# Which side of a matmul the weights take: gate sections and branch projections of a hybrid retention and attention step

## The chip, the cores and the metric

The kernel runs on one core of one Trainium2 chip. The metric is the time of one execution in device microseconds (us). A core has TensorE (PE, with PEld for the load of a stationary side), VectorE (DVE), ScalarE (ACT), GpSimd (POOL), SyncE (SP, which issues the DMAs here), a scratch memory of 128 partitions, and PSUM banks that matmuls write.

## The reference, cut to what matters

One layer runs over 640 tokens of 1024 channels: 128 of a prompt and 512 latent ones. The part that the change touches is the mixer. The experts follow it.

```python
def mixer(h, ...):
    rq, rk, rv, rg, dq, dk, dv, gr, gd = jnp.split(h @ w_in, IN_SPLITS, axis=-1)
    ...
    ret_out = (silu(rg) * o_r) @ w_ret_o          # o_r: retention, normed
    ...
    diff_out = o_d.reshape(B, T, DIFF_V_W) @ w_diff_o   # o_d: differential attention, 8 heads, normed
    merged = jax.nn.sigmoid(gr) * ret_out + jax.nn.sigmoid(gd) * diff_out
    return merged @ w_o, dk, dv, s_f, s_b

# trunk_layer
x = x + g1 * mix
h2 = rmsnorm(x, n2) * (1.0 + sc2) + sh2
x = x + g2 * hier_moe(h2, ...)    # 32 experts, two for each token
```

## The kernel before

**Tiles and products.** The tokens are five tiles of 128 (NT; tile PT = 4 is the prompt). A weight matrix of 1024 rows is read in sections of 512 columns (SECTIONS: rq ... gr0, gr1, gd0, gd1, dq1, dk1, dv1, wr0, wr1, wd0, wd1, wo0, wo1), each in two half sections of 256 columns (hh). One half section is 1 MB, has two buffers in turn, and is split for precision: ScalarE casts it to fp32r (w_high, L1366), VectorE subtracts that from the original (w_low, L1729); the plan calls the pair "cv". The left sides h (normed input), o (retention), od (attention) and m (merged) are split in the same way into whole, high (L1339) and low (L1668), the plan's "split". A left side is made from transposes of four 128x128 blocks on TensorE ("T4", L915), copied out of PSUM with a scale per channel.

A product (plan: "mm", section, tile, half) is 24 matmuls at L882: for each of eight slices of 128 input channels high by high, high by low and low by high. The stationary side is the transposed tile of tokens, the moving side 256 columns of weights, and the result has the tokens on the partitions. Products and T4s alternate between two PSUM banks, so each waits for the copy of the one before the last.

**The order.** A list written by hand, `plan` (L357 to L468), sets the order, and each engine walks through it in its own queue. The function attention(half, work) (L402) handles four of the eight heads in 20 steps, one for each head and tile: scores of this step ("S"), transposes of the probabilities of the last step ("AT", L1050, copied at L1400), then the items of `work` that fall to this step, the preparation of the next head (three T4s in a head's steps 1 to 3), and the product with the values of the last step ("PV", L1066). Behind the scores VectorE takes the maxima (L1793 to L1795), ScalarE the exponentials (L1393). `work` is spread evenly over the 20 steps by its number of products:

```python
share[max(k - 1, 0) * len(mine) // products].append(item)
```

The first half (414 to 603 us) has the 40 products of gr and gd as its work. ScalarE takes their tanh (L1324), and SP stores each result, 128 KB, in a DRAM buffer (gate_out, L654). Then come the sections dq1, dk1, dv1 (to 690 us). The second half (to 845 us) has the 20 products of wr, with the o splits of tile t+1 behind the first section's product of tile t. SP brings back a gate for each (load_gate, L662), and VectorE writes (1 + tanh) x product into `merge` (L1636). At the end of wr1 SP asks for all gates of the attention branch at once, 2.5 MB (gd_t, L755).

**Behind the attention** (att_end, where SP also asks for the residual rows and the experts 0 and 1) stand the od transposes, those of tiles 0 and 1 ahead and those of 2 to 4 between the first five products of wd; then the rest of wd, where VectorE multiplies with the gate and adds to `merge` (L1646, L1649). The gated-merge tiles are then transposed in the same way (ten T4s, "m", with the factor 0.5) between the first products of wo; then wo1, the router, and 32 experts whose weights arrive by DMA. At the last product of wo1 SP asks for the experts 2 and 3 (L758). A product of w_o that opens the section waits for its tile's splits:

```python
if s in ("rq", "wr0", "wd0", "wo0") and hh == 0:
    pe.wait_ge(x_split, split_n[(kind, t, 1)])
```

The function final_engine (L471) gives the copy out of PSUM to ScalarE or VectorE: wr, wd and wo to VectorE, T4s of left sides by turns.

## Time and profile before

| | us |
|---|---|
| median of 3 runs (lowest, highest) | 1314.54 (1313.31, 1319.37) |
| the profiled execution | 1315.77 |
| its span in the profile | 1313.9 |
| TensorE busy | 1131.1 |
| VectorE busy | 495.6 |
| ScalarE busy | 403.5 |
| GpSimd busy | 92.4 |

The span runs from the first to the last recorded instruction of the profiled execution. "Busy" is the time in which an engine worked on an instruction that the profile counts. The chain of waits is followed back from the last instruction, each time to what released it. A bracket behind an instruction of a timeline gives the idle time before it and the instruction that ended it.

### The profile page before, as it was taken

Reading aid. Unit: us, or ns where it says so; the run is one execution under the profiler, and the core shown is the slowest. Engines: PE = TensorE matmul, PEld = TensorE weight load, DVE = VectorE, ACT = ScalarE, POOL = GpSimd, SP = SyncE. Lnnn points to the kernel's source line nnn. Section 1 sums busy time; section 2 is a strip of 40 time slices with the busy share of each in tenths; the row PEclk is TensorE's granted clock in tenths of the full one; section 3 lists DMA queues with packets and bytes.
Section 4 is the critical chain, followed back from the end, with each engine's and each line's share of the span. In section 5 each row is a group of like instructions: output and inputs, shape, how many; then the busy total and the mean of one; then the engine's idle time right before and its main releaser. Section 6 shows DMA issues by size and latency. Waiting matters only on the chain.

```text
span 1313.9 us, 19321 instructions
## 1 busy us (share of the span) xinstructions
PE 1131.1 (86%) x8087; PEld 916.5 (70%) x8087; DVE 495.6 (38%) x897; ACT 403.5 (31%) x870; POOL 92.4 (7%) x103
## 2 busy tenths in 40 slices
PE   2799999989998999999998888799895789777773
PEld 0488899989987888899996777699895333222221
DVE  0531114573343443442526545445547311111116
ACT  2532222211233545453225544421322121111113
POOL 0000001121000000000000000000001111110001
PEclk9799999999999999999999999899998799999996
DMA  8555632221321231223222111481316989999956
GB/s 302 220 170 204 224 98 65 65 60 46 105 65 41 61 93 61 75 80 109 65 73 69 53 48 49 158 319 65 129 33 254 381 346 419 421 421 421 421 241 240
DMA packets 90276, 222.32 MB, mean 169 GB/s; under 512 B 9881, under 2 KB 64962, under 8 KB 74706
## 3 DMA queue, kind: packets, MB, share of 16 engines
q1 hardware_dynamic: 85298, 209.60, 43.6%
q0 software_dynamic: 4608, 10.49, 2.1%
q8 instruction: 61, 1.00, 0.3%
q10 hardware_dynamic: 288, 1.05, 0.2%
q14 instruction: 21, 0.17, 0.0%
HBM read 206.40 MB, written 21.00 MB: 173 GB/s over the span
## 4 chain that ended last, share of the span: by engine, by line
PE 61%; DMA 13%; DVE 8%; ACT 8%; issue 6%; SPq 2%; POOL 1%; ACTq 0%; DVEq 0%; POOLq 0%
PE ps L882 39%; DMA arena<-in_moe_w_up 8%; PE ps L1112 6%; PE ps L1036 3%; PE ps L1066 3%; ACT arena L1393 2%; PE ps L1125 2%; DMA w_loaded<-in_w_in 2%; ACT w_high L1366 2%; DVE w_low L1729 2%; PE ps L1050 1%; PE ps L849 1%; DVE mx L1793 1%; DVE mx L1794 1%; DMA w_loaded<-in_w_diff_o 1%
## 5 line engine op out<-in xcount | busy, mean ns | idle before, releaser
L882 PE MATMUL ps<-w_high,h_high 128*128 128x256 f32 x1280 | 371.2, 290 | 10.0 <-DVE arena L1626 5.2
L882 PE MATMUL ps<-w_low,h_high 128*128 128x256 f32 x1280 | 364.5, 285 | 0.0
L882 PE MATMUL ps<-w_high,h_low 128*128 128x256 f32 x1280 | 364.4, 285 | 0.0
L882 PEld LDWEIGHTS ps<-w_high,h_high 128*128 128x128 f32 x1280 | 248.0, 194 | 24.5 <-ACT arena L1333 10.1
L882 PEld LDWEIGHTS ps<-w_low,h_high 128*128 128x128 f32 x1280 | 248.0, 194 | 0.2
L882 PEld LDWEIGHTS ps<-w_high,h_low 128*128 128x128 f32 x1280 | 247.8, 194 | 0.0
L1729 DVE TENSOR_TENSOR w_low<-w_loaded,w_high 128x2048 fp32r<-128x2048 f32 x44 | 100.8, 2291 | 177.7 <-ACT w_high L1366 177.7
L1112 PE MATMUL ps<-arena 128*64 128x512 f32 x512 | 121.3, 629 | 24.3 <-DMA arena<-in_moe_w_up 17.0
L1333 ACT COPY arena<-ps 128x256 f32<-128x256 f32 x100 | 37.2, 372 | 251.8 <-PE ps L882 251.8
L1112 PEld LDWEIGHTS ps<-arena 128*64 128x64 f32 x512 | 40.0, 145 | 103.5 <-issue 103.5
L1366 ACT CAST w_high<-w_loaded 128x2048 fp32r<-128x2048 f32 x44 | 84.0, 1908 | 62.0 <-DMA w_loaded<-in_w_o 37.4
L1393 ACT ACTIVATE arena<-ps,neg_mx 128x768 f32<-128x768 f32 (+1 forms) x80 | 62.8, 790 | 106.3 <-DVE neg_mx L1795 106.3
L1125 PE MATMUL ps<-arena 128*64 128x512 f32 x256 | 58.4, 598 | 9.8 <-ACT arena L1441 9.8
L1066 PE MATMUL ps<-arena 128*128 128x128 f32 x384 | 49.3, 278 | 13.3 <-ACT arena L1400 13.3
L1920 DVE SCALAR_TENSOR_TENSOR arena<-arena,ps 128x256 f32<-128x256 f32 x16 | 6.7, 421 | 141.1 <-ACT arena L1437 141.1
L1793 DVE TENSOR_REDUCE mx<-ps 128x1 f32<-128x768 f32 (+1 forms) x40 | 32.9, 822 | 71.5 <-PE ps L1036 71.5
L1066 PEld LDWEIGHTS ps<-arena 128*128 128x128 f32 x384 | 45.5, 192 | 16.1 <-ACT arena L1400 16.1
L1036 PE MATMUL ps<-arena 64*128 64x256 f32 (+2 forms) x288 | 53.9, 488 | 2.5 <-ACT arena L1282 1.5
L915 PE MATMUL ps<-const,arena 128*128 128x128 f32 x256 | 41.8, 294 | 11.2 <-POOL arena L2042 3.5
L882 PE MATMUL ps<-w_high,od_high 128*128 128x256 f32 x160 | 47.8, 299 | 4.1 <-DVE arena L1646 2.8
L882 PE MATMUL ps<-w_high,m_high 128*128 128x256 f32 x160 | 46.3, 289 | 2.0 <-DVE m_low L1668 0.8
L882 PE MATMUL ps<-w_high,o_high 128*128 128x256 f32 x160 | 46.9, 293 | 0.8 <-DVE o_low L1668 0.8
(268 smaller groups left out, 1664.0 us busy)
## 6 DMA issues: line engine op xcount, KB each, us to landing
w_loaded<-in_w_in SPq DMA_DIRECT2D x32, 1024.0 KB, 5.6
arena<-in_moe_w_gate SPq DMA_DIRECT2D x32, 1024.0 KB, 14.2
arena<-in_moe_w_up SPq DMA_DIRECT2D x32, 1024.0 KB, 20.5
arena<-in_moe_w_down SPq DMA_DIRECT2D x32, 1024.0 KB, 21.0
arena<-in_w_ada SPq DMA_DIRECT2D x24, 1024.0 KB, 5.7
gates<-arena SPq DMA_DIRECT2D x40, 128.0 KB, 1.7
arena<-y_rows SPq DMA_DIRECT2D x10, 512.0 KB, 8.2
arena<-in_x_sample SPq DMA_DIRECT2D x8, 512.0 KB, 10.8
```

The lines of the kernel that those rows point to most:

```text
L849: mm = pe.matmul(B(7)[32 * j:32 * j + 32, :], ccol[:, k, :], ada_place[ada_slot(i)][:, j * N512:(j + 1) * N512], start=(k == 0), stop=(k = ...
L882: mm = pe.matmul(out[:, 0:N256], x[:, t, k * P:(k + 1) * P], w[i % 2][:, k, :], start=(k == 0 and j == 0), stop=(k == KC - 1 and j == 2))
L915: mm = pe.transpose(out[:, k * P:(k + 1) * P], src[k], ident)
L1036: mm = pe.matmul(score[c][:, lo:hi], qT[h % 2][r, t * P:(t + 1) * P], keys, start=True, stop=True, skip_group_check=True)
L1066: mm = pe.matmul(pv_out, mixedT[s % 2][:, k * P:(k + 1) * P], v, start=(k == 0), stop=(k == 5))
L1112: mm = pe.matmul(B(bank_at)[BLK * i:BLK * (i + 1), :].rearrange("p (g f) -> p g f", g=2), xgT[slot][:, k, BLK * i:BLK * (i + 1)], w_gu[e0 ...
L1125: mm = pe.matmul(B(5 + n)[BLK * i:BLK * (i + 1), :], act_aT[slot][:, k, BLK * i:BLK * (i + 1)], w_dn[e0 + i][:, k, n * N512:(n + 1) * N512 ...
L1333: free(act.copy(dst[:, t, c0:c0 + N256], src), n)
L1366: act.copy(w_hi[i % 2][:], w_raw[i % 2]).then_inc(w_rounded, 1)
L1393: act.activation(probs[:, c, 0:n], score[c][:, 0:n], ACT.Exp, bias=neg_mx[:, s % 2, c:c + 1], scale=DH ** -0.5, accum_out=den[:, s % 2, c: ...
L1729: dve.tensor_tensor(w_lo[i % 2][:], w_raw[i % 2], w_hi[i % 2][:].bitcast(F32), ALU.subtract).then_inc(w_split, 1)
L1793: dve.tensor_reduce(mx[:, 0:1], score[0][:, 0:n], AXX, ALU.max)
```

## The change

Four kinds of section (gr, gd, wr, wd) swap the sides: 128 channels of weights are the stationary side and tokens move, 320 and 320 of them (in wd 384 and 256). A half section then has four products of 24 matmuls instead of five, and the results have channels on the partitions. The function block_of gives the channel block and the tokens of a product. The gates in DRAM, gd_t and `merge` take this layout (a gate store or load is 160 KB), so that `merge` is m's whole form: m has no T4s, its high and low parts are made from `merge` with the factor 0.5, one piece behind each product of wd.

In the plan, `work` is spread by a weight of 5 for a product and 2 for a T4. The o splits of tiles 0 to 2 stand ahead of the second half of the attention, those of tiles 3 and 4 behind its first product. The od T4s of heads 0 to 3 (half 0) with their splits become the last items of the attention's second half; the others stand behind it, ahead of the first product of wd (tiles 0 to 2) and behind it (3 and 4). The matmuls of a product are in the order high by high, low x by high w, high x by low w. The scale and shift rows of the second norm are asked for at the end of wd1 instead of behind the last m T4. Some buffers move to other places of the arena (a gate buffer holds 320 columns; scale2, shift2, h2, the weights of one expert slot, the gathered rows and the router's scratch lie elsewhere).

```diff
-        for kind, whole_kb, high_kb in (("h", 158, 118), ("o", 138, 118), ("od", 118, 178), ("m", 178, 138)):
-            left[kind] = (split_at(kind + "_whole", whole_kb, NT, D, F32), split_at(kind + "_high", high_kb, NT, D),
-                          split_at(kind + "_low", whole_kb, NT, D))
-        rv, gd_t = tiles(138, NT, D), tiles(138, NT, D)
+        for kind, whole_kb, high_kb in (("h", 158, 118), ("o", 138, 118)):
+            left[kind] = (split_at(kind + "_whole", whole_kb, KC, TOK, F32), split_at(kind + "_high", high_kb, KC, TOK),
+                          split_at(kind + "_low", whole_kb, KC, TOK))
+        merge = cols_of(158)
+        left["m"] = (merge, split_at("m_high", 138, KC, TOK), split_at("m_low", 158, KC, TOK))
+        left["od"] = (split_at("od_whole", 118, NT, D, F32), split_at("od_high", 178, NT, D), split_at("od_low", 118, NT, D))
+        rv, gd_t = tiles(138, NT, D), cols_of(138)
...
-        gates_dram = nc.dram_tensor("gates", [2, P, NT, D], F32).ap()
+        gates_dram = nc.dram_tensor("gates", [2, P, KC, TOK], F32).ap()
...
+        BY_COLUMN = ("gr", "gd", "wr", "wd")
+        LAST = lambda s: 3 if s[:2] in BY_COLUMN else PT
+
+        def block_of(s, j, hh):
+
+            lo, n = ((0, 3 * P), (3 * P, 2 * P))[j % 2] if s[:2] == "wd" else (TH * (j % 2), TH)
+            return 4 * int(s[2]) + 2 * hh + j // 2, slice(lo, lo + n), n
...
-            for t in range(NT):
+            for t in range(LAST(s) + 1):
                 out.append(("mm", s, t, hh))
-                if t == 2 and i + 1 < len(UNITS):
+                if t == LAST(s) // 2 and i + 1 < len(UNITS):
...
-            products = sum(item[0] == "mm" for item in work)
+            weight = lambda item: 5 if item[0] == "mm" else 2 if item[0] == "T4" else 0
+            products = sum(weight(item) for item in work)
             share, k = [[] for _ in mine], 0
             for item in work:
-                k += item[0] == "mm"
-                share[max(k - 1, 0) * len(mine) // products].append(item)
+                share[min(max(k, 0) * len(mine) // products, len(mine) - 1)].append(item)
+                k += weight(item)
...
+        half_of = lambda what, t, half: [("T4", what, t, half), ("split", what, t, half)]
         split_o = lambda t: [("split", "o", t, half) for half in range(2)]
-        for item in split_o(0):
+        for t in range(3):
+            for item in split_o(t):
+                emit(item)
+        first = unit("wr0", 0)
+        first[1:1] = split_o(3) + split_o(4)
+        attention(1, first + unit("wr0", 1) + section("wr1") + [x for t in range(NT) for x in half_of("od", t, 0)])
+        plan.append(("att_end",))
+        opening = unit("wd0", 0)
+        opening[1:1] = half_of("od", 3, 1) + half_of("od", 4, 1)
+        m_piece = None
+        for item in [x for t in range(3) for x in half_of("od", t, 1)] + opening + unit("wd0", 1) + section("wd1"):
             emit(item)
-        first = []
-        for item in unit("wr0", 0):
-            first += [item] + (split_o(item[2] + 1) if item[0] == "mm" and item[2] + 1 < NT else [])
-        attention(1, first + unit("wr0", 1) + section("wr1"))
-        plan.append(("att_end",))
-        for n, item in enumerate(with_left("od", unit("wd0", 0)) + unit("wd0", 1) + section("wd1")):
-            emit(item)
-            if item[0] == "mm" and item[1:] in (("wd0", 1, 1), ("wd0", 2, 1), ("wd0", 3, 1), ("wd0", 4, 1)):
-                plan.append(("W", item[2] - 1))
-            if item == ("mm", "wd1", 2, 0):
-                plan.append(("LB",))
-        for item in with_left("m", unit("wo0", 0)) + unit("wo0", 1):
+            if item[0] == "mm":
+                if m_piece:
+                    emit(m_piece)
+                m_piece = ("split", "m", block_of(*item[1:])[0], item[2] % 2)
+                if item[1] == "wd0" and item[3] == 1:
+                    plan.append(("W", item[2]))
+                if item == ("mm", "wd1", 2, 0):
+                    plan.append(("LB",))
+        emit(m_piece)
+        for item in section("wo0"):
             emit(item)
...
+        def splits_needed(s, t):
+
+            if s == "rq":
+                return split_n[("h", t, 1)]
+            if s == "wo0":
+                return split_n[("m", KC - 1, 0 if t < 3 else 1)]
+            what, tiles_in = ("o" if s == "wr0" else "od"), (range(3) if t % 2 == 0 else range(NT))
+            return max(split_n[(what, u, half)] for u in tiles_in for half in range(2))
+
+        def piece(what, v, t, half):
+
+            if what == "m":
+                sl = (slice(0, 3 * P), slice(3 * P, TOK))[half]
+                return v[:, t, sl]
+            if what == "od":
+                return v[:, t, N512 * half:N512 * (half + 1)]
+            return v[:, 4 * half:4 * half + 4, t * P:(t + 1) * P]
...
-                    elif item == ("T4", "m", PT, 1):
+                    elif n == last_of["wd1"]:
...
-                        pe.wait_ge(x_split, split_n[(kind, t, 1)])
+                        pe.wait_ge(x_split, splits_needed(s, t))
                     _, x_hi, x_lo = left[kind]
+                    _, sl, width = block_of(s, t, hh) if s[:2] in BY_COLUMN else (0, slice(t * P, (t + 1) * P), N256)
                     for k in range(KC):
-                        for j, (x, w) in enumerate(((x_hi, w_hi), (x_hi, w_lo), (x_lo, w_hi))):
-                            mm = pe.matmul(out[:, 0:N256], x[:, t, k * P:(k + 1) * P], w[i % 2][:, k, :],
-                                           start=(k == 0 and j == 0), stop=(k == KC - 1 and j == 2))
+                        for j, (x, w) in enumerate(((x_hi, w_hi), (x_lo, w_hi), (x_hi, w_lo))):
+                            if kind == "od":
+                                tokens = x[:, sl.start // P:sl.stop // P, k * P:(k + 1) * P]
+                            else:
+                                tokens = x[:, k, sl]
+                            if s[:2] in BY_COLUMN:
+                                fixed, moving = w[i % 2][:, k, (t // 2) * P:(t // 2 + 1) * P], tokens
+                            else:
+                                fixed, moving = tokens, w[i % 2][:, k, :]
+                            mm = pe.matmul(out[:, 0:width] if kind != "od" else out[:, 0:width].rearrange("p (t n) -> p t n", n=P),
+                                           fixed, moving, start=(k == 0 and j == 0), stop=(k == KC - 1 and j == 2))
...
-                wait_freed(act, where[("T4", what, t, half)])
-                c = slice(N512 * half, N512 * (half + 1))
-                act.copy(left[what][1][:, t, c], left[what][0][:, t, c]).then_inc(x_rounded, 1)
+                whole, high = piece(what, left[what][0], t, half), piece(what, left[what][1], t, half)
+                if what == "m":
+                    act.wait_ge(merged, merged_at[(t, half)])
+                    scale_copy(high, whole, 0.5).then_inc(x_rounded, 1)
+                else:
+                    wait_freed(act, where[("T4", what, t, half)])
+                    act.copy(high, whole).then_inc(x_rounded, 1)
...
-                    c0 += N256 * hh
+                    cb, sl, _ = block_of(s, t, hh)
                     dve.wait_ge(ld_gr[v % 4], 16 * (v // 4 + 1))
-                    free(dve.scalar_tensor_tensor(out=merge[:, t, c0:c0 + N256], in0=gate_t[:, v % 4, :], scalar=1.0,
-                                                  in1=src[:, 0:N256], op0=ALU.add, op1=ALU.mult), n)
+                    free(dve.scalar_tensor_tensor(out=merge[:, cb, sl], in0=gate_t[:, v % 4, :], scalar=1.0,
+                                                  in1=src[:, 0:TH], op0=ALU.add, op1=ALU.mult), n)
                 elif kind == "wd":
-                    c0 += N256 * hh
+                    cb, sl, width = block_of(s, t, hh)
                     dve.wait_ge(pe_dense, n + 1)
                     dve.wait_ge(ld_gd, 16)
-                    m = merge_t[:, n % 2, :]
+                    m = gated[:, 0:width]
                     if n_merged[0]:
                         dve.wait_ge(merged, n_merged[0])
                     n_merged[0] += 1
-                    free(dve.scalar_tensor_tensor(out=m, in0=gd_t[:, t, c0:c0 + N256], scalar=1.0, in1=src[:, 0:N256],
+                    free(dve.scalar_tensor_tensor(out=m, in0=gd_t[:, cb, sl], scalar=1.0, in1=src[:, 0:width],
                                                   op0=ALU.add, op1=ALU.mult), n)
                     wait_freed(dve, n)
-                    dve.tensor_tensor(merge[:, t, c0:c0 + N256], merge[:, t, c0:c0 + N256], m, ALU.add).then_inc(merged, 1)
+                    dve.tensor_tensor(merge[:, cb, sl], merge[:, cb, sl], m, ALU.add).then_inc(merged, 1)
...
-                c = slice(N512 * half, N512 * (half + 1))
-                whole, high, low = left[what]
-                dve.tensor_tensor(low[:, t, c], whole[:, t, c], high[:, t, c].bitcast(F32), ALU.subtract).then_inc(x_split, 1)
+                whole, high, low = (piece(what, v, t, half) for v in left[what])
+                if what == "m":
+                    dve.scalar_tensor_tensor(out=low, in0=whole, scalar=0.5, in1=high.bitcast(F32), op0=ALU.mult,
+                                             op1=ALU.subtract).then_inc(x_split, 1)
+                else:
+                    dve.tensor_tensor(low, whole, high.bitcast(F32), ALU.subtract).then_inc(x_split, 1)
```

## Rows read from the trace of the kernel before

**Rows 1.** page, section 1: engine, busy us, share of the span, instructions

```profile
PE 1131.1 (86%) x8087; PEld 916.5 (70%) x8087; DVE 495.6 (38%) x897; ACT 403.5 (31%) x870; POOL 92.4 (7%) x103
```

**Rows 2.** stretches from:to in us: length, busy us of each engine, granted clock, DMA

```profile
414.00:603.00 189.00, 181.80 (x1445) 165.43 (x1444) 78.34 (x128) 92.46 (x236) 7.92 (x9) 1.00 0.24 70
...
690.00:845.00 155.00, 129.99 (x972) 109.45 (x972) 81.87 (x154) 79.11 (x208) 8.53 (x11) 1.00 0.17 56
...
1121.00:1276.00 155.00, 119.76 (x532) 44.16 (x532) 17.26 (x29) 22.49 (x47) 16.19 (x16) 0.96 0.95 394
```

**Rows 3.** the chain that ended last: start us, length us, engine, line, instructions

```profile
203.47 1.73 PE ps L929 x8
603.14 86.40 PE ps L882 x720
```

**Rows 4.** timeline at 74.7 us, after a stall: start us, length us, engine, line

```profile
74.72 0.38 PE L882 MATMUL ps<-w_high,h_high 128*128 128x256 f32 x1
74.82 0.19 PEld L882 LDWEIGHTS ps<-w_low,h_high 128*128 128x128 f32 x1
74.94 0.28 PE L882 MATMUL ps<-w_low,h_high 128*128 128x256 f32 x1
```

**Rows 5.** timeline of TensorE where transposes follow a product

```profile
704.47 0.28 PE L882 MATMUL ps<-w_high,o_low 128*128 128x256 f32 x1
704.58 0.60 PE L915 MATMUL ps<-const,arena 128*128 128x128 f32 x4
```

**Rows 6.** the chain: first product of w_diff_o

```profile
850.81 5.39 PE ps L882 x24
```

**Rows 7.** timeline of a step in the first half: scores, copy for PV

```profile
489.17 1.56 PE L1036 MATMUL ps<-arena 64*128 64x512 f32 x8
...
495.07 0.39 ACT L1400 COPY arena<-ps 128x256 f32<-128x256 f32 x1
```

**Rows 8.** the chain in the second half of the attention

```profile
689.94 1.04 ACT o_high L1339 x2
...
692.91 1.58 PE ps L1036 x8
...
707.74 1.51 PE ps L1036 x8
...
727.11 2.88 PE ps L882 x24
...
737.50 1.51 PE ps L1036 x8
...
745.47 1.51 PE ps L1036 x8
```

**Rows 9.** timelines behind the last head: transposes, copy out, cast, subtraction

```profile
847.42 3.04 PE L915 MATMUL ps<-const,arena 128*128 128x128 f32 x12 [3.54 <-POOL arena L2042]
848.54 0.75 DVE L1597 TENSOR_SCALAR od_whole<-ps,cols 128x512 f32<-128x512 f32 x1 [2.39 <-PE ps L915]
849.32 0.62 ACT L1339 CAST od_high<-od_whole 128x512 fp32r<-128x512 f32 x1 [3.90 <-DVE od_whole L1597]
849.98 0.69 DVE L1668 TENSOR_TENSOR od_low<-od_whole,od_high 128x512 fp32r<-128x512 f32 x1 [0.68 <-ACT od_high L1339]
```

**Rows 10.** the chain at w_diff_o's third quarter, and TensorE's timeline there

```profile
873.10 12.80 DMA w_loaded<-in_w_diff_o
...
890.54 10.19 PE ps L882 x72
...
890.54 0.58 PE L882 MATMUL ps<-w_high,od_high 128*128 128x256 f32 x1 [2.48 <-DVE arena L1646]
```

**Rows 11.** the chain from the last products of w_diff_o through w_o

```profile
900.91 20.20 PE ps L882 x168
...
925.69 3.12 PE ps L882 x24
...
945.65 14.67 PE ps L882 x120
```

79 lines of the change are left out of this document (39 added, 40 removed).

## The prediction

> **What bounds the kernel now.** I read the page first, for shares: TensorE is busy for 86% of the span [rows 1]. That is a mean over stages with different limits, so I cut the trace into stretches [rows 2]. In the first half of the attention (414 to 603 us), where the gate sections lie between the steps, TensorE is busy for 181.8 of 189 us: it is the bound there. In the second half (690 to 845 us) it is busy for 130 of 155 us, and the chain of waits runs through the softmax (VectorE's maxima, ScalarE's exponentials and copies). From 1121 to 1276 us, in the experts, DMA moves 394 GB/s and sets the pace. The loads of the experts 2 and 3 are released by the last product of w_o, and the change does not touch what comes after, so the end moves by as much as that product moves. The reader is to see that a matmul saved counts in the first half of the attention and in the projections, and that in the second half only the chain counts.
>
> **What one matmul costs.** 720 matmuls of 256 columns took 86.40 us: 120.0 ns each, where 256 columns at 2.4 GHz are 106.7 ns [rows 3]. After a stall the second weight load starts 0.10 us after the first matmul's stamp and the second matmul 0.22 us after it [rows 4]: the load needs 0.10 to 0.11 us, and the columns then some 0.12. The transposes behind such a matmul start 0.11 us after it as well [rows 5]. So the 120 ns belong to the moving side rather than to the load. Two readings fit these rows: 13.3 ns once per matmul, or 0.469 ns per column. No other width of this type is in the trace. For 320 columns they give 133.3 + 13.3 = 146.6 ns, or 150 ns. Plain fp32 products of 256 columns, two cycles each, took 216 ns, 2.9 over their 213.3 [rows 3]; with that surcharge 320 columns would take 136.2. So the bounds are 136 and 150. The change needs 96 matmuls of 320 for 120 of 256 in each half section, the same columns. I take 146.6, because the half clock shows the bare 213 ns (24 in 5.39 us with the last one's tail [rows 6]), as a fixed cost in another clock would.
>
> The Trainium skill (TensorE: Matmul & The Clock Gate, Back-to-back issue gap) gives N/2.4 + 2.5 ns at full clock. For 256 that is 109 ns, and the trace says 120, so the rule as it stands does not hold for these products. For 320 it would be 135.8 ns, and the time that of the second rival below.
>
> **Gate sections (first half of the attention).** Forty products of 24 matmuls become 32: 960 x 0.1200 = 115.2 us become 768 x 0.1466 = 112.6, so -2.6. The items are shared out by weight now, 8 in 5 steps, so two steps of five have one instead of two. In a full step the copy that PV waits for ends 6.3 us after the scores start [rows 7]; scores, transposes, one product (3.5) and the preparation make some 6.1, so such a step loses about 0.2, four times: +0.8. ScalarE has 8 tanh fewer and the stores of the gates are 160 KB instead of 128, both off the path. Total -1.8 (bounds +0.8 and -9).
>
> **Opening of the second half.** The first product of w_ret_o now takes tokens 0 to 319, so six pieces of the split are queued ahead of the key and query copies on ScalarE, where there were two. Two took 1.04 us of the chain [rows 8], so four more are +2.1.
>
> **The second step.** The product for tokens 320 to 639 needs the pieces of tiles 3 and 4, and the plan puts these four behind the exponentials of the same step. Ahead of them stand maxima, exponentials and copies, 6.3 us; then four pieces at 0.52 on ScalarE (1.04 for two [rows 8]) and VectorE's last subtraction (0.7): the product starts about 9.6 us after the scores. With 3.5 for it, 0.4 for the preparation and 1.5 for PV the step is 15.1 us long. Before, the scores of steps one and three stand at 692.91 and 707.74 [rows 8], with 5.6 for the first step and 9.2 for the second. That is +5.9. Step four loses two pieces on the chain: -1.0. TensorE stands still for some 7 us in that step; at half clock the product would take 24 x 0.267 = 6.4 instead of 3.5, so between 0 and +2.9. After 3.5 us without work, up to 847.42 [rows 9], the clock was at 1.2 GHz [rows 6], so I take +2.
>
> **The other steps.** Ordinary steps are 7.97 us (737.50 to 745.47 [rows 8]); 3.5 us of product fit beneath the chain where 2.88 did. In the short step of a head the product is itself on the chain (727.11, 2.88 us [rows 8]): 3 heads x 0.64 = +1.9.
>
> **Last head.** Ten transpose groups of the first half of od now stand in its last four steps in place of four products: each brings a copy out of PSUM (0.7), a cast (0.6, ScalarE) and a subtraction (0.7, VectorE) [rows 9]. They are queued ahead of the read of PV, on which the next transposes wait. With three groups in a step the third also needs the bank of the first, ahead of PV. Walked through by these durations the four steps become longer by 1.1, 0, 2.1 and 1.4; the weight split that moves into the step ahead of them costs 0.8: +5.4. Bounds: 0, if all fits in idle slots, and +8.
>
> **Projection w_diff_o.** Start: three groups must be ready instead of one, so the first product comes 6.6 us after the transposes begin instead of 3.4 [rows 6, 9]: +3.2. First half section: 22.3 us before (850.81 to 873.10 [rows 6, 10]), with six transpose groups between the products. After: 384 columns at 173 ns, 24 of them, with 2.2 for the half clock as before [rows 6], 6.4; then a gap of 4.8 for two groups with their splits; then 2.9 + 4.2 + 2.9: 21.2, so -1.1. Before, the weights asked for at 873.10 landed 12.8 us later behind expert loads, and TensorE waited 2.5 us, until 890.54, and then ran at half clock for a while (72 products in 10.19 us, 1.5 over 72 x 0.12) [rows 10]. The 2.5 MB of gates are now loaded four steps earlier, off this queue, so I take the wait and the half clock as gone: -4.0. The three half sections that follow take 14.1 us each instead of 14.4: -1.0. Total -2.9 (bounds +4 and -8).
>
> **Projection w_o.** The merged product has its channels on the partitions, so ten transpose groups go. Before: 921.11 (end of the products) to 925.69, then 19.96 us to 945.65 for 14.4 us of products [rows 11]. After: the last merge (0.9) and one subtraction (0.6) with their waits, some 1.8, then 14.4. That is -2.8 and -5.6: -8.4. The scale rows are loaded earlier, and nobody waits for them.
>
> **Sum.** -1.8 + 2.1 + 5.9 - 1.0 + 2.0 + 1.9 + 5.4 - 2.9 - 8.4 = +3.2 us. The profiled execution took 1315.77 us (span 1313.9, 1.9 around it), 1.2 above the median of the runs. Against the median: 1314.5 + 3.2 = 1317.7 us.
>
> **Rivals.**
> First, slower: the cost goes by columns (150 ns for 320) and the half clock comes at each new gap. The gates then give back nothing (2.6 worse), the projections 1.3 less, and the clock costs 1 more in step two and some 2 in the opening and the 4.8 us gap: 3.2 + 6.9 = +10.1, 1324.6 us. It decides if 320 columns take over 148 ns. For it: two times 256 columns cost double in every stretch. Against it: the half clock shows no surcharge per column.
> Second, faster: the 13.3 ns come from a clash with the weight load, which 320 columns outlast, and 136 ns are left, the surcharge of plain fp32 [rows 3]. The gates give -9.7 instead of -1.8 (768 x 14.2 = 10.9 less than at 150, of which the chain in the one-product steps takes back 1.2), the short steps cost 0.7 less, the projections give 2.1 more: 3.2 - 10.7 = -7.5, 1307.0 us. Against it: a load that is over after 0.11 us, and the spacing of 0.11 to 0.12 ahead of a transpose, whose load is shorter [rows 4, 5].
> Third, the waits of the second half are hidden better than I walked through: the clock stays up in step two (-2) and the od groups fall into idle slots (-5.4): 1310.3 us. For it: ScalarE is busy for 79 of 155 us there [rows 2]. Against it: its queue is in order, and the pieces stand ahead of what the chain waits for.
>
> **How the numbers follow.** Forecast 0.42, first rival 0.28, second 0.14, third 0.16. About 0.5% (6.6 us) is what a measurement of this kernel can tell from no change: faster ends at 1308, slower begins at 1321. Faster takes most of the second rival and a third of the third (0.17), slower nearly the whole first and a quarter of the forecast (0.35), no change the rest (0.48). The range takes in all four cases with what their unknown costs leave open: 1304 to 1327.
>
> **What would show it.** The spacing of matmuls of 320 columns: 147, 150 or 136 ns. The second step of the second half 15 us or longer, with TensorE idle until o_low. The last four steps some 5 us longer in sum. From the end of w_diff_o's products to the first of w_o under 2 us, and no transposes behind. No wait for w_diff_o's third quarter. I would be wrong if TensorE waited for the gates' stores or loads, or if the expert loads began at another distance from the last product of w_o.

## The result

| | before | changed kernel |
|---|---|---|
| median of 17 runs each (lowest, highest), us | 1314.54 (1311.69, 1319.84) | 1319.29 (1316.56, 1322.25) |
| ratio to the kernel before, 95% interval | | 1.0035 (1.0025 to 1.0045) |
| the profiled execution, us | 1315.77 | 1318.80 |
| its span, us | 1313.9 | 1317.0 |

The change makes the kernel 4.8 us slower, 0.35%. The forecast was 1317.7 us, 1.6 below the measured median, with no change as the likeliest case. The prediction called no change what lies within 0.5% (1308 to 1321 us), and 1319.3 lies there; with 17 runs of each kernel the interval still excludes no change. Ratios here and below are worked out over the fast runs and are not the quotients of two medians. The page of the changed kernel, section 1 (engine, busy us, share, instructions), answers to [rows 1]:

```profile
PE 1128.4 (86%) x7663; PEld 913.0 (69%) x7663; DVE 491.8 (37%) x886; ACT 401.4 (30%) x863; POOL 93.7 (7%) x103
```

It says next to nothing: 424 matmuls fewer, and all shares within one point of what they were. The chain of waits says where the time went. The changed kernel's (start us, length us, engine, line, instructions; L1089 are the scores, L938 the products):

```profile
413.58 1.56 PE ps L1089 x8
...
443.67 7.04 PE ps L938 x48
...
454.23 3.52 PE ps L938 x24
...
597.35 86.40 PE ps L938 x720
684.14 3.11 ACT o_high L1393 x6
689.64 2.93 PE ps L1089 x8
692.57 4.56 PE ps L938 x24
...
704.11 1.38 DVE o_low L1723 x3
706.66 5.92 PE ps L938 x24
...
714.36 1.51 PE ps L1089 x8
...
868.12 6.17 PE ps L938 x24
878.88 36.83 PE ps L938 x240
...
934.45 29.05 PE ps L938 x240
...
973.32 3.10 PE ps L938 x24
```

Three more lines of the same view of the kernel before, beside those of the rows 3, 6, 8 and 11: the first scores, a cast that stands in the chain once in a head, and the first product of w_o's second section.

```profile
415.20 1.56 PE ps L1036 x8
...
450.82 1.42 ACT w_high L1366
...
969.76 3.10 PE ps L882 x24
```

The differences of these starts, cut at the same events, beside the terms of the forecast:

| stretch | before | after | difference | forecast |
|---|---|---|---|---|
| start to the first scores | 415.2 | 413.6 | -1.6 | 0 |
| to the first product of dq1 (gate sections) | 187.9 | 183.8 | -4.2 | -1.8 |
| to the first scores of the second half | 89.8 | 92.3 | +2.5 | +2.1 |
| to the first product of w_diff_o | 157.9 | 178.5 | +20.6 | +17.4 |
| to the first product of w_o | 74.9 | 66.3 | -8.5 | -8.9 |
| to the first product of wo1 | 44.1 | 38.9 | -5.2 | -5.6 |
| to the end of the span | 344.1 | 343.7 | -0.5 | 0 |
| sum | | | +3.1 | +3.2 |

Nothing in the first stretch was changed. Its length lay between 410.8 and 416.2 us in the fourteen kernels of this study, so the 1.6 us there are chance. They are also the gap between the +3.1 of the two profiled executions and the +4.8 of the medians. That the last row comes out as +3.1 and +3.2 is luck: the largest misses in the rows above are -1.6, -2.4 and +3.2 us, and they nearly cancel.

So the change gives 18 us back where it was meant to, in the gates and the projections, and the second half of the attention takes 20.6 us of it. The experiments are about these 20.6 us.

### The profile page after: what moved, and what is told of

It reads as the page before. It is cut to its first block, busy times and chain, and to the rows that moved or that the text cites. A ratio compares the mean times of both kernels' runs of the same rounds, so it can differ in the third digit from the quotient of the medians.

```text
span 1317.0 us, 18423 instructions
## 1 busy us (share of the span) xinstructions
PE 1128.4 (86%) x7663; PEld 913.0 (69%) x7663; DVE 491.8 (37%) x886; ACT 401.4 (30%) x863; POOL 93.7 (7%) x103
## 4 chain that ended last, share of the span: by engine, by line
PE 64%; DMA 12%; DVE 7%; issue 7%; ACT 6%; SPq 2%; POOL 1%; ACTq 0%; DVEq 0%; POOLq 0%
PE ps L938 42%; DMA arena<-in_moe_w_up 8%; PE ps L1165 6%; PE ps L1089 4%; PE ps L1119 3%; PE ps L1178 2%; ACT arena L1447 2%; DMA w_loaded<-in_w_in 2%; PE ps L1103 1%; PE ps L896 1%; ACT w_high L1420 1%; DVE mx L1848 1%; DVE mx L1849 1%; DVE w_low L1784 1%; PE ps L968 1%
## 5 line engine op out<-in xcount | busy, mean ns | idle before, releaser
L938 PE MATMUL ps<-w_high,h_high 128*128 128x256 f32 x960 | 278.5, 290 | 10.4 <-DVE arena L1678 5.2
L938 PE MATMUL ps<-w_high,h_low 128*128 128x256 f32 x960 | 273.5, 285 | 0.0
L938 PE MATMUL ps<-w_low,h_high 128*128 128x256 f32 x960 | 273.4, 285 | 0.0
L938 PEld LDWEIGHTS ps<-w_high,h_high 128*128 128x128 f32 x960 | 186.1, 194 | 24.5 <-ACT arena L1383 10.1
L938 PEld LDWEIGHTS ps<-w_high,h_low 128*128 128x128 f32 x960 | 186.3, 194 | 0.2
L938 PEld LDWEIGHTS ps<-w_low,h_high 128*128 128x128 f32 x960 | 186.1, 194 | 0.0
L938 PE MATMUL ps<-h_high,w_high 128*128 128x320 f32 x256 | 80.7, 315 | 0.0
L938 PE MATMUL ps<-h_high,w_low 128*128 128x320 f32 x256 | 79.1, 309 | 0.0
L938 PE MATMUL ps<-h_low,w_high 128*128 128x320 f32 x256 | 79.1, 309 | 0.0
L1848 DVE TENSOR_REDUCE mx<-ps 128x1 f32<-128x768 f32 (+1 forms) x40 | 33.0, 824 | 85.6 <-PE ps L1089 85.6
L1119 PE MATMUL ps<-arena 128*128 128x128 f32 x384 | 52.6, 290 | 12.3 <-ACT arena L1454 11.9
L1119 PEld LDWEIGHTS ps<-arena 128*128 128x128 f32 x384 | 48.3, 201 | 16.2 <-ACT arena L1454 16.1
L1089 PE MATMUL ps<-arena 64*128 64x256 f32 (+2 forms) x288 | 57.7, 517 | 1.5 <-ACT arena L1335 1.5
L938 PE MATMUL ps<-o_high,w_high 128*128 128x320 f32 x128 | 42.4, 331 | 9.1 <-DVE o_low L1723 7.2
```

The lines of the kernel that those rows point to most:

```text
L938: mm = pe.matmul(out[:, 0:width] if kind != "od" else out[:, 0:width].rearrange("p (t n) -> p t n", n=P), fixed, moving, start=(k == 0 and ...
L1089: mm = pe.matmul(score[c][:, lo:hi], qT[h % 2][r, t * P:(t + 1) * P], keys, start=True, stop=True, skip_group_check=True)
L1119: mm = pe.matmul(pv_out, mixedT[s % 2][:, k * P:(k + 1) * P], v, start=(k == 0), stop=(k == 5))
L1848: dve.tensor_reduce(mx[:, 0:1], score[0][:, 0:n], AXX, ALU.max)
```

## The experiments

The starts of the scores on TensorE's timeline give the length of each step of the attention's second half. Here they are in us (steps are counted from the first of the half; "5 to 16" is the sum of these twelve; steps 17 to 19 are the last head's second to fourth, and "opening" is from its last scores, those of step 20, to the first product of w_diff_o; step 3 is 7.88 in every kernel):

| kernel | step 1 | 2 | 4 | 5 to 16 | 17 | 18 | 19 | opening | first product of w_diff_o |
|---|---|---|---|---|---|---|---|---|---|
| before | 5.59 | 9.17 | 9.75 | 85.5 | 7.97 | 7.88 | 8.71 | 15.45 | 850.82 |
| changed | 7.42 | 17.23 | 9.11 | 86.1 | 10.92 | 10.50 | 9.05 | 20.31 | 868.12 |
| e1, o splits early | 5.69 | 8.03 | 9.11 | 86.1 | 10.57 | 8.27 | 9.12 | 20.31 | 852.39 |
| e2, od behind | 7.21 | 17.12 | 9.12 | 81.7 | 7.98 | 7.88 | 9.12 | 19.86 | 856.84 |
| e3, long fill, last steps | 7.22 | 17.12 | 9.12 | 86.1 | 12.18 | 10.33 | 9.87 | 21.54 | 873.56 |
| e4, long fill, step 2 | 7.48 | 18.30 | 9.12 | 86.1 | 11.82 | 8.79 | 8.96 | 20.32 | 869.25 |
| e9, half fill, both | 6.80 | 16.54 | 9.12 | 86.1 | 10.58 | 7.88 | 7.88 | 19.81 | 859.06 |
| e7, e1 and e2 together | 5.68 | 8.04 | 9.11 | 83.3 | 7.98 | 7.88 | 9.11 | 17.97 | 843.62 |

### The o splits ahead of the second half

```diff
         for s in ["dq1", "dk1", "dv1"]:
             for item in section(s):
                 emit(item)
+                if item[0] == "mm" and item[1] == "dv1" and item[3] == 1 and item[2] < PT:
+                    for piece_of in split_o(item[2]):
+                        emit(piece_of)
-        for t in range(3):
-            for item in split_o(t):
-                emit(item)
-        first = unit("wr0", 0)
-        first[1:1] = split_o(3) + split_o(4)
```

The splits of the last tile go to attention(1) as a list that it emits behind its three preparation groups.

> The changed kernel, with the o splits of tiles 0 to 3 behind the products of the same tiles in the last half section of dv1 and those of tile 4 behind the preparation of the second half of the attention. Theory (what the second step and the opening lost is the wait for the pieces of the split, with the half clock that follows): from the first product of dq1 to the first scores of the second half 92.3 us become some 88.8; these scores take 1.6 us instead of 2.9 and the first product 3.5 instead of 4.6 (-1.8); the second step falls from 17.2 us to 9.2 to 9.8. In sum -12 to -13.5 us, some 1306.5, which is 0.6% below the kernel before. Rival (ScalarE and VectorE have no room for ten more pieces beside the sections): TensorE waits in dv1 for the copies out of PSUM, and the maxima of the second step stand behind o_low: half of the gain or less, 1313.

Measured: 1303.56 us against 1314.71 for the kernel before on the same chip, ratio 0.9931 (0.9906 to 0.9956), and 15.7 us below the changed kernel. Two stretches of its trace (from:to, length, busy us of PE, PEld, DVE, ACT and POOL, granted clock, DMA share, GB/s), and one of the changed kernel:

```profile
687.30:701.00 13.70, 13.07 (x86) 10.91 (x86) 8.70 (x16) 6.06 (x14) 0.00 (x0) 1.00 0.40 135
823.00:852.00 29.00, 15.03 (x80) 11.41 (x79) 12.64 (x24) 13.71 (x36) 2.63 (x3) 0.74 0.31 120
```

```profile
689.60:714.30 24.70, 17.42 (x88) 14.41 (x88) 10.09 (x18) 7.15 (x15) 0.00 (x0) 0.77 0.08 25
```

Steps 1 and 2 are the first line of the new kernel (13.7 us, clock 1.00) and the line of the changed kernel (24.7 us, clock 0.77). The theory held, and by more than it had said: the second step is shorter than before the change, 8.03 us, because before it carried pieces of the split too. From the first product of dq1 to the scores it took 88.9 us (forecast 88.8). Not all of the 15.7 us belongs to the splits: step 18, which the edit does not touch, fell from 10.50 to 8.27 us. The second line is the last head, where the clock is still down (0.74), only at other moments. What the clock does there is the next section's matter. The same edit on the kernel before:

> The kernel before with the same edit of the o splits (tiles 0 to 3 behind the products of dv1, tile 4 behind the preparation). Theory (before the change the pieces stood beside work and only the two of tile 0 and those in the second and fourth step were on the chain): -1.0 for the opening, -1.1 for the second step (9.17 to 8.0), -0.6 for the fourth: some -3, 1311.7. So of the 11 us by which the changed kernel with this edit is faster than the kernel before, 8 would belong to the change. Rival (the pieces cost before as they did behind the change): -8 or more, 1306.

Measured: 1312.49 us, ratio 0.9979 (0.9966 to 0.9992), -2.2 us; up to the first scores of the half -0.9, second step 7.97 instead of 9.17, fourth 8.71 instead of 9.75. The opening of w_diff_o is 1.1 us longer, and why stays open. So the pieces cost little where the left side is cut by tiles, since each product needed one tile, and much where a product needs three or five tiles at once. With the same edit in both, the changed kernel (1303.56) is 8.9 us faster than the kernel before (1312.49).

### What the clock costs

```diff
+                for _ in range(FILL_ITEM.get(item, 0)):
+                    pe.matmul(out[:, 0:P], ident, ident, start=True, stop=True)
```

> The changed kernel with small plain fp32 matmuls (identity by identity) on TensorE where it stood still in the last head: 20 behind the last product of w_ret_o, 28, 24 and 10 ahead of the od groups of the last steps, 24 ahead of the first group behind the attention and 20 ahead of the first product of w_diff_o. They are no part of the computation. Clock theory (the last steps are long because TensorE, idle there, falls to 1.2 GHz, and the scores then take 2.8 us instead of 1.6, the product with the values 2.9 instead of 1.6, the first product of w_diff_o 6.2 instead of 4.2): -4 to -6 us, 1314.5, and the granted clock of the stretch from 826 us to the first product of w_diff_o near 1. Queue theory (they are long because the copies and splits of the od groups stand ahead of what the chain waits for, as the prediction walked through): no gain, and up to 2 us lost.

> The changed kernel with 48 small plain fp32 matmuls (5.3 us, no part of the computation) on TensorE in the second step of the second half, ahead of the wait for the o pieces of tiles 3 and 4. Clock theory: the 7.2 us in which TensorE stood still are what took its clock down, so the product behind them takes 3.5 us instead of 5.9: the step falls from 17.2 to 14.9 us, -2.4, 1317. If the clock does not come from this gap: no change, or up to 5 us slower where the added matmuls themselves run at 1.2 GHz.

Measured: 1320.74 us (ratio 1.0045, 1.0028 to 1.0062) and 1319.03 us (1.0025, 1.0014 to 1.0037): no gain, and both sizes were mine to get wrong. One such matmul is two instructions and took 0.22 us, not 0.11. The chain of the first, then of the second:

```profile
834.19 6.25 PE ps L920 x56
...
873.80 4.19 PE ps L942 x24
```

```profile
700.36 10.72 PE ps L920 x96
711.08 3.51 PE ps L942 x24
```

28 of them, ahead of the first od group, took 6.25 us where 3.5 us were free, and 48 took 10.7 where 7.2 were free. What they were to show, they show: with fill ahead of it, the first product of w_diff_o took 4.19 us instead of 6.17 (384 columns), and the product of the second step 3.51 instead of 5.92 (320 columns). The same at half the length:

> The fills of the two earlier kernels again, at half their length, since one such matmul took 0.22 us and not 0.11: 24 in the second step (5.3 us), and in the last head 9 behind the last product of w_ret_o, 13, 12 and 5 ahead of the od groups, 11 and 10 behind the attention. They are no part of the computation. Clock theory: the second step takes 14.9 us instead of 17.2; with the scores at 1.6 us and the products with the values at 1.6 us, the first step with an od group takes 8.3 us instead of 10.5, and the first product of w_diff_o 4.2 us instead of 6.2: some -6.5, 1313. Queue theory: only the second step gains (-2.4, 1317), and the last head's steps keep 10.9, 10.5 and 9.1 us although their scores and products run at 2.4 GHz.

Measured: 1310.60 us, ratio 0.9957 (0.994 to 0.9974), 8.7 us below the changed kernel, by work that computes nothing. TensorE's timeline in steps 18 and 19 (L920 is the fill, L972 the od transposes, L1128 the product with the values, L1093 the scores), then, here and in the changed kernel, the stretch from the product with the values ahead of step 18's scores to the first product of w_diff_o:

```profile
828.59 0.60 PE L972 MATMUL ps<-const,arena 128*128 128x128 f32 x4
829.83 1.60 PE L1128 MATMUL ps<-arena 128*128 128x128 f32 x12 [0.64 <-ACT arena L1463]
831.37 1.56 PE L1093 MATMUL ps<-arena 64*128 64x512 f32 x8
832.86 0.88 PE L1107 MATMUL ps<-const,arena 128*128 128x128 f32 x6
833.57 2.84 PE L920 MATMUL ps<-const 128*128 128x128 f32 x24
```

```profile
821.90:859.00 37.10, 28.39 (x223) 24.58 (x223) 17.43 (x32) 17.67 (x46) 2.63 (x3) 1.00 0.46 179
```

```profile
826.40:868.10 41.70, 23.80 (x121) 18.07 (x122) 17.38 (x32) 17.64 (x46) 2.63 (x3) 0.72 0.42 166
```

The chain of the changed kernel in the same place has the products with the values (L1119) and the scores (L1089) at 1.9 to 2.9 us instead of 1.6:

```profile
826.39 1.94 PE ps L1119 x12
828.33 2.82 PE ps L1089 x8
...
835.90 2.93 PE ps L1119 x12
838.83 2.68 PE ps L1089 x8
```

With the clock at 1.00, steps 18 and 19 take 7.88 us each, the first exactly as before the change and the second less: the od groups of these two steps, their copies and splits included, cost nothing on the chain. They took the place of products, and TensorE, left without work for 2.6, 3.5 and 3.1 us at a time, fell to 1.2 GHz.

Step 20 is not like that. Its scores start 12.05 us ahead of the transposes behind the attention in the kernel before, 13.6 us in this one with its clock at 1.00, and 13.6 us in the changed kernel. There the od pieces do stand ahead of the chain in ScalarE's queue: L1393 is their cast, L1314 the read of the product with the values. In the kernel before, that read (L1261) stands right behind the product (L1066).

```profile
840.06 1.35 PE ps L1066 x12
...
841.44 0.37 ACT arena L1261
```

```profile
855.15 0.62 ACT od_high L1393
855.77 0.27 ACT arena L1314
856.03 0.36 ACT ps L1464 x2
```

Step 17 is a third kind: it stays at 10.58 us with the clock up. VectorE's timeline of the changed kernel shows why (the bracket is the idle time before):

```profile
818.70 2.29 DVE L1784 TENSOR_TENSOR w_low<-w_loaded,w_high 128x2048 fp32r<-128x2048 f32 x1 [0.48 <-ACT w_high L1420]
820.91 0.48 DVE L1688 SCALAR_TENSOR_TENSOR arena<-arena,ps 128x320 f32<-128x320 f32 x1
821.31 0.95 DVE L1848 TENSOR_REDUCE mx<-ps 128x1 f32<-128x768 f32 x1
```

The scores of step 17 were done at 818.9, and their maxima (L1848) start at 821.3, behind the weight split (w_low) that the new share put into step 16, the short first step of the head. That the weight split makes step 17 long is read from this timeline; the next section has a kernel in which it lies elsewhere, though not that alone was moved.

In the second step the half clock went only in part: the fill ended 1.8 us before the product, which then took 5.3 us instead of 5.9.

The changed kernel's clock also does not fall at one fixed moment: e4, which differs from it only in step 2, has 11.82 and 8.79 us in steps 17 and 18 where the changed kernel has 10.92 and 10.50.

### The od groups behind the attention

```diff
-        attention(1, first + unit("wr0", 1) + section("wr1") + [x for t in range(NT) for x in half_of("od", t, 0)])
+        attention(1, first + unit("wr0", 1) + section("wr1"))
-        opening[1:1] = half_of("od", 3, 1) + half_of("od", 4, 1)
+        opening[1:1] = [x for half in range(2) for t in (3, 4) for x in half_of("od", t, half)]
-        for item in [x for t in range(3) for x in half_of("od", t, 1)] + opening + unit("wd0", 1) + section("wd1"):
+        for item in [x for half in range(2) for t in range(3) for x in half_of("od", t, half)] + opening + unit("wd0", 1) + section("wd1"):
```

> The changed kernel with all ten od transpose groups behind the attention, those of heads 0 to 3 first (they need nothing of the last head), and the work of the second half spread without them. Theory (the groups in the last steps cost what these steps became longer by, 5.9 us in the steps before the last, and the wait for GpSimd behind the last product with the values, 3.8 us, has room for the three groups of half 0): the last head's steps are back at 8.0, 7.9 and 8.7 us, the first product of w_diff_o starts at the same distance behind the last product with the values, and the gap behind that product grows by two groups (+2.1). In sum -3 to -5 us, 1315. Rival (the groups are only moved: each costs its 1.05 us on the copying engines wherever it stands, and here nothing hides them): +5.3 against -5.9, no change, 1319.

Measured: 1311.68 us, ratio 0.9971 (0.9956 to 0.9987), 7.6 us below the changed kernel. Steps 17 to 19 are at 7.98, 7.88 and 9.12 us. The opening is not longer, 19.86 us against 20.31, with six transpose groups in it instead of five: the three of half 0 stand beside GpSimd's work on the last head. The gap behind the first product grew from 4.9 to 8.2 us (862.6 to 870.85 between starts), more than the 2.1 expected.

This edit does a second thing, which neither theory had. The work of the half is now spread without the groups, so the sixteen products fall on other steps, and none of them on a head's short step, that of the prompt (steps 5, 10 and 15: 4.41 us each). In the changed kernel only step 10 is free of one, and steps 5 and 15 take 6.60 us. Steps 5 to 16 are 4.4 us shorter in sum. So the trace has 5.5 us of gain in steps 17 to 19, 0.4 in the opening and 4.4 in the middle of the half, against 3.3 us lost behind the first product. The weight split, too, falls elsewhere (VectorE runs it at 828.1 us, in step 19). Step 17, which held a product but no od group in the changed kernel, takes 7.98 us without it, 2.6 less than in e9. That bears out the reading of step 17 above.

> The two edits together: o splits early (alone 1303.6) and all od groups behind the attention (alone 1311.7), on the changed kernel (1319.3). Theory (the two costs lie in different stretches and have nothing in common): they add up, -15.7 and -7.6, 1296.0. Rival (each also pays for the same half clock in the last steps, which fell from 10.5 to 8.3 us in the first of them): some 2 to 3 us less, 1298.5.

Measured: 1298.09 us, ratio 0.9865 (0.984 to 0.989). That is 2 us above the plain sum, where the rival had put it: both edits had won the same time in steps 17 and 18 (0.3 and 2.2 us). Two other differences nearly cancel: the opening is 1.9 us shorter than in e2, and steps 10 and 11 are 1.6 us longer (5.22 and 6.97 instead of 4.41 and 6.17), with the granted clock at 0.83 and 0.88 there. The clock fell there in e10 as well, and not in e2 and e12.

### What a matmul costs by its width

```diff
+        TIMED = {"gr0": 448, "gr1": 192, "gd0": 128, "gd1": 512}
+                            if s in TIMED:
+                                width, moving = TIMED[s], x[:, k, 0:TIMED[s]]
```

> The changed kernel with other widths of the moving side in the gate sections: 448 columns in gr0, 192 in gr1, 128 in gd0, 512 in gd1, instead of 320 (only the first 320 of the result are used, so the gates are not the reference's). In the changed kernel 320 columns take 146.6 ns and before the change 256 took 120.0. Fixed cost per matmul (13.3 ns beside 0.4167 ns per column): 200.0, 93.3, 66.7 and 226.7 ns. Cost by columns (0.469 ns): 210, 90, 60 and 240 ns. If the weight load, some 0.10 us after a stall, bounds the narrow ones: 105 to 120 ns for 128 and for 192.

One run took 1334.25 us; only the spacing of its matmuls is of use here. The chain, one pair of products of each width, in the order 448, 192, 128, 512:

```profile
427.07 9.73 PE ps L941 x48
...
497.37 5.34 PE ps L941 x48
...
539.92 5.31 PE ps L941 x48
...
554.55 10.94 PE ps L941 x48
```

Medians between starts are 203, 111, 111 and 227 ns, with 120, 147 and 173 ns for the 256, 320 and 384 columns of the other sections. From 256 up that is 13.3 ns and 0.4167 ns per column, within 3 ns (200.0 for 448, 226.7 for 512); below, it stands at 111 ns. The Trainium skill (TensorE: Matmul & The Clock Gate, LDWEIGHTS) has P/1.2 ns for a load of P stationary columns, 106.7 for 128; the floor of 111 ns agrees with a load that bounds the narrow ones, which no run here separates from another floor.

### The wait for the third quarter of w_diff_o

The forecast had put its end down to the gates, which are loaded earlier. The first kernel for it asked for them in `att_end` behind a wait for the last product of w_ret_o:

> The changed kernel with the load of the 2.5 MB of gates asked for behind the last step of the attention, where the kernel before had it, instead of four steps earlier. Theory of the prediction (the wait for the third quarter of w_diff_o went because the gates left the queue ahead of it): that load lands 4 to 6 us later than now, TensorE waits 1 to 3 us at the third half section and runs at half clock for a while behind it: +2 to +4 us. Rival (the wait went because this load is now asked for 16 us behind the last expert load instead of 6): no wait there, no change.

One run took 1319.33 us, and it tells nothing: SyncE waited for nothing else there and asked at 824.7 us instead of 824.3. The second waits for the last product with the values:

```diff
+                    sp.wait_ge(pe_pv, 40)
+                    sp.dma_start(gd_t, gates_dram[1]).then_inc(ld_gd, 16)
                     residual()
```

> The changed kernel with the load of the 2.5 MB of gates asked for only when the last product with the values is done, ahead of the residual rows and the expert loads. The earlier kernel with this aim did not move it: SyncE waits there for nothing but the last product of w_ret_o, and asked for it at 824.70 us of the span, as in the changed kernel at 824.25. Here it is asked for some 33 us later. Theory of the prediction (the wait for the third quarter of w_diff_o went because the gates left the queue ahead of it): 2.5 MB at some 420 GB/s are 6 us more ahead of the experts' 6 MB, so the third quarter's load lands 9 to 11 us behind its request instead of 5.2, and TensorE waits 0 to 2 us for it. Rival (it went because this request now comes 16 us behind the last expert load instead of 7): it still lands within 6 us, and no wait.

The view of the tile w_loaded, its last line (from request to landing; the longest is the third quarter), in the kernel before, the changed kernel and this one:

```profile
DMA to landing us min/median/max: 5.0/5.1/12.8
```

```profile
DMA to landing us min/median/max: 5.0/5.1/5.3
```

```profile
DMA to landing us min/median/max: 5.0/5.1/9.7
```

One run of this kernel took 1321.82 us. The load lands after 9.7 us, as the theory said, and between the second and the third half section TensorE's starts lie 0.74 us apart instead of 0.12. So the gates' place is worth 4.4 us of the 7.5 by which the landing came earlier, but only 0.6 us of TensorE's wait. Not all of the 4.4 need be the gates' own bytes: the later request also put the last expert load 6.7 us later (880.81 instead of 874.10), 10.3 us ahead of the third quarter's request. The other 3.1 us are argued from SyncE's timeline, not tested: the third quarter was asked for 7 us behind the last expert load before (866.10 and 873.10) and is now asked for 16 us behind it (874.10 and 890.48).

### A shorter opening

```diff
-            lo, n = ((0, 3 * P), (3 * P, 2 * P))[j % 2] if s[:2] == "wd" else (TH * (j % 2), TH)
+            lo, n = ((3 * P, 2 * P), (0, 3 * P))[j % 2] if s[:2] == "wd" else (TH * (j % 2), TH)
...
+        def staggered(groups):
+            t4s, splits_of = [("T4", "od", t, half) for t, half in groups], [("split", "od", t, half) for t, half in groups]
+            return t4s[:1] + [x for pair_of in zip(t4s[1:], splits_of) for x in pair_of] + splits_of[-1:]
+        opening[1:1] = staggered([(2, 0), (0, 1), (1, 1), (2, 1)])
...
+        for item in staggered([(3, 0), (4, 0), (0, 0), (1, 0), (3, 1), (4, 1)]) + opening + unit("wd0", 1) + section("wd1"):
```

> The two edits of the last call together (1298.1), and the opening of w_diff_o made shorter: its products take tokens 384 to 639 first and 0 to 383 second, so the first product needs two tiles of od instead of three; and each group's split stands behind the next group's transposes, so that ScalarE and VectorE do not wait for each other at every group. Theory (the opening is bound by the two copying engines, which in the present order take 3.28 us for two groups where their own work is 2.15): the first product starts some 4 us earlier and the gap behind it falls from 8 to about 4.5 us: -6 to -7, 1291.5. Rival (the wait for GpSimd or the half clock bounds the opening): -2 or less, 1296.

Measured: 1293.73 us, ratio 0.9838 (0.982 to 0.9856), -4.4 us against the last one where -6 to -7 were expected. The opening is 15.3 us (825.33 to 840.61) instead of 18.0, the gap behind the first product 6.2 us instead of 8.2, and 1.0 us is lost again ahead of w_o (2.8 us from the start of the last matmul of w_diff_o instead of 1.8), where the first product now waits for the larger of the last two m pieces.

> The last kernel (1293.7) with small plain fp32 matmuls, no part of the computation, in three gaps of the opening of w_diff_o: 5 ahead of the transposes of the first group of half 1, 12 ahead of the first product, 10 ahead of the second. Clock theory: the first product (256 columns) takes 2.9 us instead of 4.6 and the second (384) 4.2 instead of 5.7: -3, 1290.7. Rival (the clock is down already ahead of them, or the added matmuls run over into the time of the products): no gain, or up to 2 us slower.

Measured: 1291.07 us, ratio 0.9812 (0.9779 to 0.9846). The first product of w_diff_o in its chain:

```profile
837.94 3.13 PE ps L946 x24
```

In the kernel without fill that product's starts span 4.6 us (840.61 to 845.22), here 2.8 (837.94 to 840.77), and from the first product of w_diff_o to the first of w_o it is 3.1 us less. That agrees with the 3 us that the fill had been given. The times of the runs support it less firmly: the medians differ by 2.7 us, but the two intervals overlap, and the kernel without fill has in its trace the slow steps 10 and 11 (+1.6 us) that this one has not. This is the fastest kernel of the study, 23 us below the kernel before on the same chip.

## Why the prediction was right, point by point

**What one matmul costs: right.** 320 columns took 146.6 ns and 384 took 173, the numbers of the sum. The first rival (150 by columns) and the second (136) fall with it. The rule N/2.4 + 2.5 of the Trainium skill (TensorE: Matmul & The Clock Gate, Back-to-back issue gap) does not hold for these fp32r products: it gives 215.8 ns for 512 columns, and 227 were measured.

**Gate sections: -4.2 against -1.8.** The mis-sized term is the one-product step. I let four of them lose 0.2 us; one took 7.88 us, where 9.83 less 2.24 of product is 7.59, so each lost 0.3. What I had not looked at is the prompt step of a head. It went from 9.68 to 6.60 us, 0.83 more than the product gives. In the kernel before, ScalarE casts a weight there (450.82, the line above) ahead of the copies that the chain waits for, and TensorE stands still for 1.32 us behind the scores; with eight items in five steps the cast falls elsewhere, and it stands still for 0.48. Three such steps are 2.5 us, which is the whole miss. This is read from the timelines; no run tests it.

**Opening and second step: right, but for the first scores.** 92.3 us against 91.9, and 17.2 us for the second step against 15.1 and 2 for the clock. Its product started 9.6 us behind the scores (697.06 to 706.66), as forecast, though the terms that the prediction lists for it add up to 9.1. The clock was down at the first scores already (2.93 us instead of 1.58, and 4.56 for the first product), which cost 1.8 us that the forecast had not (only the first rival let the clock fall in an opening).

**Other steps: +0.5 against +1.9.** The short step costs the 0.64 that I gave it, twice, but 16 products and five groups over 20 steps leave the third short step without a product (4.41 us instead of 5.96). A long step costs 0.40 more in two of the heads (9.12 instead of 8.72), which I had not.

**Last head: within its bounds, the working wrong.** The forecast was +5.4 for the last four steps and +3.2 for the start of w_diff_o, +8.6; measured are +5.9 in steps 17 to 19 (2.95, 2.62 and 0.34) and +4.9 in the opening, +10.8. Of the opening, 3.3 us are the start of w_diff_o, as forecast, so the last head is +7.5. The prediction speaks of ten transpose groups of half 0, three of them in one step; the diff emits five, one to two in a step. And it charged them to the queues of ScalarE and VectorE. That is right for step 20 alone: 1.4 us forecast, some 1.5 measured with the clock up. In steps 18 and 19 the fill at half length showed them to cost nothing. What was in their place: the weight split ahead of step 17's maxima, put at 0.8 and worth 2.6 (10.58 in e9 less 7.98 in e2); and the half clock behind TensorE's missing products, 2.6 us in step 18 and 1.2 in step 19, where the missing product gives 0.8 back. The half clock in the first product of w_diff_o is no part of this: the forecast had it, and the kernel before has it too. So queues that were charged too much hid a clock that was charged nothing, and that the sum came near is luck. The third rival (the groups fall into idle slots) had the mechanism right for steps 18 and 19 and still not the time, since it let the clock stay up.

**w_diff_o and w_o: right, the cause of one term in part.** The distance from the transposes of half 1 to the first product was 6.7 us (861.45 to 868.12; forecast 6.6), the gap behind it 4.9 (4.8). The first half section took 22.2 us instead of 21.2, since the second product ran its first part at half clock. The wait for the third quarter went, as forecast, with the cause only in part the gates. From the last product of w_diff_o to the first of w_o 1.7 us (forecast 1.8), and no transposes behind.

## What to carry to other kernels

A wider moving side saves what a matmul costs beside its columns, here 13.3 ns of 120; that is worth something only if the wider operand is there in time, because one product now needs three or five tiles where it had needed one. So with the change move the work that makes the operand: the same change with its splits ahead and its transposes behind the attention is 1.35% faster than the kernel before, and as it stood it was 0.35% slower. (Splits ahead give the kernel before 0.2% too, and part of the gain is the new spread of the products: fewer products than steps are best kept out of the steps in which a product is on the chain.) And where a plan takes matmuls out of a chain-bound stage, count the clock as a cost of the gap they leave: a step can become longer by having less to do.

## What the runs showed of the hardware

- fp32r products with 128 stationary columns: 111 ns between starts for 128 and 192 moving columns, 120 for 256, 147 for 320, 173 for 384, 203 for 448, 227 for 512 at 2.4 GHz; at 1.2 GHz 213 for 256, 267 for 320 and 320 for 384, with nothing beside the columns.
- A plain fp32 matmul of 128 columns is two instructions, 0.22 us together.
- TensorE doing nothing of use can shorten a kernel: 8.7 us by 84 idle matmuls in the changed kernel, and some 3 us (by the trace; the intervals of the times overlap) by 27 in the fastest one.
- The clock fell at other moments in kernels that did the same there: steps 17 and 18 took 10.92 and 10.50 us in the changed kernel and 11.82 and 8.79 in e4; steps 10 and 11 took 1.6 us more in e7 and e10 than in e12.
